# Two gate tiles of the pool branch multiplied in slices inside the attention, in two PSUM banks taken from the scores

## The reference, cut to what matters

```
def gated_merge(h, y_a, y_b, y_c, w_g, b_gate, w_out):
    g = jax.nn.sigmoid(h @ w_g + b_gate)
    m = (g[..., :D_MODEL] * y_a + g[..., D_MODEL:2 * D_MODEL] * y_b
         + g[..., 2 * D_MODEL:] * y_c)
    return m @ w_out
```

```
def multiscale_pool(h, w_p, w_group, scale, w_proj):
    ...
    mixed = jnp.einsum('blgc,gcd->blgd', pooled, w_group).reshape(b_, l_, POOL_CH)
    return (mixed * scale) @ w_proj

def diff_attend(q, k, v, lam):
    s = jnp.einsum('bhiqd,bhikd->bhiqk', q, k).astype(jnp.float32) * (HEAD_DIM ** -0.5)
    p = jax.nn.softmax(s, axis=-1)
    a = (p[:, :, 0] - lam * p[:, :, 1]).astype(v.dtype)
    return jnp.einsum('bhqk,bhkd->bhqd', a, v)
```

## Time and profile before

| what | value |
|---|---|
| median of 3 runs | 2213.51 us (2211.35 to 2217.54) |
| profiled execution, first to last instruction | 2206.9 us |
| what lies around that span, by the median | 6.6 us |
| PE busy | 2128.5 us, 96% |
| DVE busy | 1442.9 us, 65% |
| ACT busy | 891.7 us, 40% |
| attention of layer 0 | about 271.6 to 344.8 us of the span |
| attention of layer 1 | about 1168.1 to 1213.6 us |

### The profile page before, as it was taken

The page is one execution under the profiler, slowest core; times in us unless marked ns, Lnnn a source line. Parts: engine busy times, 40 slices in busy tenths (PEclk is TensorE's granted clock), DMA queues, the critical chain, the costliest instruction groups (busy, mean ns, idle before and its releaser), DMA issues. The chain is left out here.

```text
span 2206.9 us, 32856 instructions
## 1 busy us (share of the span) xinstructions
PE 2128.5 (96%) x13074; PEld 1835.4 (83%) x13074; DVE 1442.9 (65%) x2148; ACT 891.7 (40%) x1396; POOL 178.1 (8%) x251
## 2 busy tenths in 40 slices
PE   5999999999999999999999999999999999999998
PEld 3777767888888887788886998998888998898997
DVE  3487585664567766237967676875696775566764
ACT  3222374432342222235326555444455444444443
POOL 3422000010010000004310001000100000000000
PEclk9999999999999999999999999999999999999999
DMA  8544301333326666234420564776633666543663
GB/s 286 162 142 128 112 6 58 89 93 105 123 86 182 187 207 221 92 115 131 132 86 21 162 190 151 238 222 204 179 115 89 190 194 199 153 133 111 194 202 124
DMA packets 428653, 320.81 MB, mean 145 GB/s; under 512 B 25925, under 2 KB 379702, under 8 KB 428502
## 3 DMA queue, kind: packets, MB, share of 16 engines
q1 hardware_dynamic: 425408, 310.52, 46.6%
q0 software_dynamic: 2656, 8.03, 1.3%
q10 hardware_dynamic: 438, 0.17, 0.0%
HBM read 317.62 MB, written 1.05 MB: 144 GB/s over the span
## 5 line engine op out<-in xcount | busy, mean ns | idle before, releaser
L344 DVE TENSOR_TENSOR split<-raw,split 128x1024 fp32r<-128x1024 f32 (+1 forms) x382 | 459.6, 1208 | 368.1 <-ACT split L341 367.1
L355 PE MATMUL PS<-HH,split 128*128 128x256 f32 (+1 forms) x1752 | 585.0, 334 | 4.0 <-DVE HL L2212 1.7
L357 PE MATMUL PS<-HH,split 128*128 128x256 f32 (+1 forms) x1752 | 573.7, 327 | 0.0
L356 PE MATMUL PS<-HL,split 128*128 128x256 f32 (+1 forms) x1752 | 573.5, 327 | 0.0
L341 ACT ACTIVATE split<-raw 128x1024 fp32r<-128x1024 f32 (+1 forms) x382 | 389.5, 1034 | 363.0 <-PE PS L357 325.6
L355 PEld LDWEIGHTS PS<-HH,split 128*128 128x128 f32 x1752 | 329.1, 188 | 42.5 <-issue 10.2
L356 PEld LDWEIGHTS PS<-HL,split 128*128 128x128 f32 x1752 | 329.3, 188 | 31.2 <-issue 1.0
L357 PEld LDWEIGHTS PS<-HH,split 128*128 128x128 f32 x1752 | 329.0, 188 | 31.3
L355 PE MATMUL PS<-HH,apart 128*128 128x256 f32 x800 | 228.7, 286 | 16.9 <-DVE HL L495 11.7
L356 PE MATMUL PS<-HL,apart 128*128 128x256 f32 x800 | 224.8, 281 | 0.0
L357 PE MATMUL PS<-HH,apart 128*128 128x256 f32 x800 | 224.6, 281 | 0.0
(11 more groups left out here) (340 smaller groups left out, 3076.6 us busy)
## 6 DMA issues: line engine op xcount, KB each, us to landing
raw<-in_w_in_dram SPq DMA_DIRECT2D x120, 512.0 KB, 4.2
raw<-in_w_ffn_in_dram SPq DMA_DIRECT2D x88, 512.0 KB, 4.8
raw<-in_l_w_gate_up_dram SPq DMA_DIRECT2D x88, 512.0 KB, 3.9
G<-in_w_mod_dram SPq DMA_DIRECT2D x82, 512.0 KB, 4.0
raw<-in_w_ffn_out_dram SPq DMA_DIRECT2D x44, 512.0 KB, 3.5
raw<-in_l_w_down_dram SPq DMA_DIRECT2D x44, 512.0 KB, 4.6
raw<-in_l_w_in_dram SPq DMA_DIRECT2D x28, 512.0 KB, 3.9
raw<-in_w_attn_out_dram SPq DMA_DIRECT2D x16, 512.0 KB, 4.0
```

Source lines behind the costliest of these rows:

```text
L344: eng.tensor_tensor(c["low"], c["raw"], c["high"].bitcast(F32), ALU.subtract).then_inc(low_done, 1)
L355: pe.matmul(out, a[0], b[0], start=first, stop=False)
L356: pe.matmul(out, a[0], b[1], start=False, stop=False)
L357: return pe.matmul(out, a[1], b[0], start=False, stop=last)
```

## The change

The scores rotate over four banks, 0 to 3. Banks 4 and 5 take the first two gate tiles of the pool branch, which PE multiplies within the attention, in steps of one slice (three matmuls), 16 steps for the two tiles. In layer 0: 3 steps behind the first two units' scores, 1 behind the next two, then one before `turned(i-2)` and one before `turned(i-1)` in each pair with i over 16, until all are made (pairs 18 to 28). In layer 1: 8, then 4, then two by two in the pair with i = 18, where only `weighted` is left. Behind the attention the pool branch starts with its output tiles 0 and 1 and goes on with gate tile 2. The weights are loaded in the new order: gate 0, gate 1, output 0, output 1, gate 2, output 2. DVE splits up to the second gate before it enters the attention.

```
-S_BANKS, PAIR_BANKS, ONE_PT_BANK, FOUR_O_BANK = (0, 1, 2, 3), (0, 1, 2, 3, 4, 5), (6,), (7,)
+S_BANKS, PAIR_BANKS, ONE_PT_BANK, FOUR_O_BANK = (0, 1, 2, 3), (0, 1, 2, 3), (6,), (7,)
+GATE_BANKS = (4, 5)
+EARLY_GATES = 2
...
+            early_weights, early_steps = {}, [(j, k) for j in range(EARLY_GATES) for k in range(KT)]
+
+            def gate_steps(count_):
+
+                for j, k in early_steps[:count_]:
+                    key = (L + "yc_gate", j)
+                    if k == 0:
+                        early_weights[j] = T.load(rows(w_in, 0, KT, COL_G + 2 * D + j * P, P), (KT, P), columns=n)
+                        T.open(key, GATE_BANKS)
+                    i, ws = early_weights[j]
+                    ins = multiply(pe, bank(key)[:, 0:n], cut2(ws, slice(None), k), own(k), k == 0, k == KT - 1)
+                    if k == KT - 1:
+                        T.close(ins, key)
+                        T.used(i)
+                del early_steps[:count_]
+
+            halfway = 2 * HEADS
             for i in range(0, len(us) + 4, 2):
                 if i < len(us):
                     scores(i)
...
                     mod_turn(T, pe, groups[4], FOUR_O_BANK)
+                if i == 0:
+                    gate_steps(8 if l else 3)
+                elif i == 2:
+                    gate_steps(4 if l else 1)
                 if i >= 4:
                     weighted(i - 4)
+                if i > halfway:
+                    gate_steps(2 if l else 1)
                 if 2 <= i < len(us) + 2:
                     turned(i - 2)
                 if i >= 4:
                     weighted(i - 3)
+                if i > halfway:
+                    gate_steps(2 if l else 1)
                 if 2 <= i < len(us) + 2:
                     turned(i - 1)
+            gate_steps(len(early_steps))
...
                 for j in range(KT):
-                    if number < 2 or j == 0:
+                    if (number == 1 or j == 0 or number == 0) and (number or j >= EARLY_GATES):
                         gate(j)
...
+            split_until(dve, (L + "mixed", 3))
             us = units_of[l]
```

## The result

Over 20 runs of each, the changed kernel takes 2224.02 us in the median (2215.17 to 2232.67) and the kernel before 2216.01 (2208.01 to 2222.73). The ratio is 1.0039, 95% interval 1.0027 to 1.0052: 6 to 11.5 us slower, where +1.5 was forecast. The first profile is of one execution of 2215.17 us, the shortest of its 20, with a span of 2213.3 against the 2206.9 of the kernel before. So the two traces explain 6.4 us, and what the medians lose over that has to be looked for elsewhere.

A forecast was written before the change was run, and what follows sets the result against it. PE's matmuls were taken as the bound outside the attention, whose holes made work free. Layer 0 at -1.4 and layer 1 at +2.85 gave +1.5 us on 2213.5, so 2215.0; range 2205 to 2222.

The forecast's parts named there:

- Total: Whole kernel: both layers sum to +1.5 us, giving 2215.0; other layers and the second block keep their work.
- the bank wait within the attention: Layer 0's attention: second scores of a pair wait for exponentials to free a bank; taken as nothing, bound 3 us.
- Layer 0, start: First layer's first scores: four gate steps cost 0.3 us, hole shrinks to 1.5, clock staying up returns 0.95.
- Layer 0, banks: First layer's attention: four score banks instead of six cause no wait, by 0.2 us margin; upper bound 3 us.
- Rival B: Attention: four banks are too few, scores wait in all 24 pairs; 12 us slower, 2227; chance 0.14.
- Layer 0, second half: Pairs 18 to 28: twelve gate steps of 8.3 us, partly covered by holes, lengthen the attention by 4.9 us.
- Layer 0, end: Behind the first attention: PE waits 3.3 us for MIX; gate 0 gives 1.8, gate 1 5.56, low clock costs 1.7.
- Layer 1: Second layer: start costs 3.1 us, end wins 1.75 despite a 3.3 wait for gate 2, clock costs 1.5; sum +2.85.
- The rule on the clock: A waiting TensorE falls to half clock: expected after holes of 2.54 and 4.3 us, not 2.11; 3.2 us in both layers.
- The clock behind the waits: Behind the waits for MIX and gate 2: clock near half, costing 1.7 us in layer 0 and 1.5 in layer 1.
- The page on tables: Layer 1's end: table switch taken as 1.28 us from the rows, not the page's 2.66, which would give about 2217.8.
- The page on banks: Attention scores: the page wants groups rotated over banks; four still do that, with less room than six; no price given.

The follow-up runs named there:

- rotation kept: Changed kernel, but each early gate tile still advances the seven-bank counter, so later tiles keep their earlier banks; 2219.89 against 2216.04 us, ratio 1.0017.
- the first experiments: Follow-up kernels, each timed in five rounds beside the kernel before; the first eight ran on one chip, the rest on another.

## Why the prediction was wrong

The step that failed is the sentence in "Total" that **what lies behind the branches keeps its work**. The work is the same, the banks are not. Taking four tiles out of the rotation puts the first tile of a product 1,300 us further down on the bank of the transposition ahead of it: 1.46 us of wait and mostly a clock near 0.5 over the 3.4 us behind, +3.1 to +3.3 us in seven traces and +1.7 in one, 3.3 to 4.9 in the ratios (1.0032 and 1.0039 against 1.0017), +4.6 when done alone. No rival held it either. A second term put at nothing, the bank wait within the attention, measured 1.7 us between 310 and the attention's end.

- **Layer 0, start.** Right in the number. The minimum of unit 2 is 0.46 us later than before against the first one (0.3 forecast), the hole is 0.89 us (1.5), and the scores behind it take 2.23 us instead of 3.12. By the minimum of unit 4 this layer is 0.94 us ahead, where 0.65 was forecast. The clock gave back 1.4 us and not 0.95 (the two rows named for it differ by 1.13). Four banks alone gain it too, so it is no merit of the gate steps.
- **Layer 0, banks.** Wrong in size: 0 taken, bound 3. Four banks alone cost 1.0 us at one handover, at the pair where units of 512 keys give way to 256, 1.6 us by 325 and 1.7 by the end of the attention. I had looked at the margin in an even pair, not at the change of length. Rival B's mechanism is real, its price of 12 us is not.
- **Layer 0, second half.** +4.9 forecast; the minima are level at 310 and 6.5 us late at 339, which less the 1.7 that four banks alone cost there is 4.8.
- **Layer 0, end.** Wait 3.23 us against 3.3, with the named releaser. Layer 0's sum is +0.5 us against -1.4; the banks' 1.7 explain most of the difference. In other traces of the same work the sum is up to +1.3.
- **Layer 1.** +2.75 us against +2.85, which is partly luck: the profile of before is the one of five with six banks in which the clock stayed up behind the wait of 2.11 us, and against the four others the layer costs 1.4. The start's 3.1 us was regained by moving the steps into the hole, and the wait at gate tile 2 is 3.43 against 3.3. What I didn't see is that the wait has a second lock behind the first: with the weights there earlier, the bank of gate tile 0 holds PE for 1.99.
- **The rule on the clock.** I took the clock of 1.00 behind the wait of 2.11 us as what such a wait does. The traces show both outcomes for the same wait: 1.00 once and 0.5 three times behind 2.11 (and 0.5 once behind 2.08), 0.5 three times out of three behind 2.54, and 1.00 once behind 3.30 (rotation kept):

```profile
1224.90:1228.30 3.40, 3.35 (x26) 1.00 0.26 77
```

- **The clock behind the waits.** Both stretches came, at 0.50 and 0.51. Their price of 1.7 and 1.5 was about right: 1.6 and 1.0 by the kernel that keeps PE warm. In layer 0 the stretch is 3.4 us long in some traces and 6.8 in others, which is most of the spread of that layer's cost.
- **The page on tables.** ACT_TABLE_LOAD took 1.28 us each time, as in the earlier trace rows, and not the 2.66 that the Trainium skill, "ScalarE: Activation LUTs", section "What ACT_TABLE_LOAD costs", gives with its drain; the row was the right choice.
- **The page on banks.** The Trainium skill, "Perfetto Trace Analysis", section "Matmuls", asks that independent groups rotate over the banks. I weighed that sentence for the six banks of the scores and not for the seven-bank rotation of everything else. The trace agrees with it at 1697.45, where two neighbours fell on one bank, at 1.46 us.

By term: layers +3.3 (forecast +1.5), rotation +3.1 (forecast 0), sum 6.4 as the two profiled spans differ. The medians differ by 7 to 9 us. The 1 to 2 us left are **open**. One candidate, the low stretch in the second block (below), looks unlikely by the mean granted clock that is on record for every run. In the experiments' profiles it is 0.990 or less where the stretch came and 0.991 or more where it did not. The kernel before, in the 35 runs beside the first experiments, has 15 runs at 0.991 to 0.994 (median 2209.7 us) and 20 at 0.987 to 0.990 (2216.9). The changed kernel, which has more low clock elsewhere, has a gap between 8 runs at 0.990 or 0.991 (2217.0) and 12 at 0.984 to 0.988 (2225.3). Like against like the change costs some 7 and 8 us, and the shares of runs are near each other. For the spacing of the matmuls 16 traces don't tell whether the change makes it more frequent.

## What to carry to other kernels

When tiles get banks of their own, look at who takes the banks from the shared counter behind them: a program can lose microseconds in a place that the diff doesn't touch, and the remedy is a line that advances the counter. A wait that the profile labels "issue" can be a bank wait. Here its end, 0.11 us after another engine's last read of the bank, gave it away, and a shift of the rotation alone proved it. Work moved out of a seam takes the cover from what is late there (MIX, a cast behind table loads): leave as many steps at the seam as the late thing takes, and put only the rest into holes that the trace of before shows as idle. Before a price is read from one trace, look at the same place in a second trace of the same program: here it moved by 1.3 us with nothing changed.

## What the runs showed of the hardware

**Matmul spacing at full clock has two values.** In layer 1's FFN, PE works without a gap at a granted clock of 1.00 in every trace, but the count of 256-column matmuls in 14 us is 126 in some executions and 121 in others. Changed kernel, first profile and then the repeat:

```profile
1400.00:1414.00 14.00, 14.00 (x126) 1.00 0.73 221
```

```profile
1400.00:1414.00 14.00, 14.00 (x121) 1.00 0.76 227
```

From start to start that is 113 against 118 ns, 4%, and it holds until the stretch ends. Six of the 16 traces have the longer one. In the repeat the output tiles of the FFN drift from 5.9 to 9.4 us behind those of the kernel before, between 1374 and 1461: 3.5 us with no wait in them. The same program shows both values, and so do the kernels with one layer changed. Nothing in the DMA columns of the two rows stands out. What sets it wasn't tried.

**A stretch of half clock in the second block comes in some executions only**, in 7 of the 16 profiles of this study. Windows in the profile with layer 0 alone changed, where the kernel before and the changed kernel both have 1.00:

```profile
1657.00:1664.00 7.00, 7.00 (x32) 0.50 0.00 0
1664.00:1671.00 7.00, 7.00 (x40) 0.64 0.01 2
```

The trace with only the rotation shifted, which moves nothing ahead of 1690, has it too, and its VectorE operations go from 2.4 to 8.6 us late across it. A single trace of this kernel can thus be 6 us off for a reason that no edit of it made, most of what the whole change costs. It is why the sums above are made place by place and not from spans.

**The same wait in the same work is followed by either clock.** The rows are shown above: behind layer 1's wait of 2.11 us the granted clock was 1.00 in the profile of before and 0.50 for 3.4 us in the trace with only the rotation shifted, which is the same program up to there; behind layer 0's wait of 3.2 us the low clock lasted 3.4 us in the first profile of the changed kernel and 6.8 in its repeat (0.51 from 354.9 to 361.8, from within the wait on). What decides it was not tried.
